# Wider column sums and constant matmuls at the boundaries, and a rearranged start of latent attention, in a fused float32 kernel of six transformer stages and two hybrid layers

## What is computed

```
def modulated_sublayer(x, mod, g_pre, g_post, fn, weight):
    shift, scale, gate = mod[:, 0], mod[:, 1], mod[:, 2]
    h = rmsnorm(x, g_pre) * (1.0 + scale) + shift
    y = rmsnorm(fn(h), g_post)
    return x + weight * (1.0 + gate) * y

def mla_mixer(h, w_in, q_norm, kv_norm, w_uq, w_uk, w_uv, w_o, cos, sin):
    lat = h @ w_in
    c_q, c_kv, k_r = jnp.split(lat, [Q_LORA, Q_LORA + KV_LORA], axis=-1)   # 256, 128, 32 wide
    c_q = rmsnorm(c_q, q_norm)
    c_kv = rmsnorm(c_kv, kv_norm)
    q = jnp.einsum('bsc,chd->bshd', c_q, w_uq)                             # 16 heads
    q_nope, q_rope = q[..., :QK_NOPE], q[..., QK_NOPE:]
    q_rope = apply_rope(q_rope, cos, sin) * ATTN_SCALE
    k_rope = apply_rope(k_r, cos, sin)
    ... scores of q_nope and q_rope against c_kv and k_rope, softmax, values, w_o
```

## Time and profile before

| | |
|---|---|
| runs | 3359.22, 3360.02, 3370.72 us |
| the profiled execution | 3363.93 us; its span 3362.2 us, mean granted clock of TensorE 0.942 |
| TensorE | busy 3128.6 us (93%), 14272 matmul records |
| weight loads of TensorE | 2536.9 us (75%) |
| VectorE | 1700.1 us (51%), 2715 instructions |
| ScalarE | 1158.8 us (34%), 2027 |
| GpSimd | 614.7 us (18%), 359 |
| DMA | 314.07 MB, mean 93 GB/s |
| chain that ended last | TensorE 43%, issue 42%, GpSimd 10%, VectorE 3%, DMA 1% |

### The profile page before, as it was taken

One profiled execution on the slowest core, in us unless ns is written; L12 is line 12 of the kernel. 1 busy time (PEld: TensorE's weight loads), 2 busy tenths in 40 slices (PEclk: granted clock), 3 DMA queues, 4 the chain that ended last, 5 costly groups with the idle time before them and its releaser, 6 DMA issues.

```text
span 3362.2 us, 40116 instructions
## 1 busy us (share of the span) xinstructions
PE 3128.6 (93%) x14272; PEld 2536.9 (75%) x14272; DVE 1700.1 (51%) x2715; ACT 1158.8 (34%) x2027; POOL 614.7 (18%) x359
## 2 busy tenths in 40 slices
PE   6999989999999998688999999996999989879999
PEld 5888878888878887466788877875777878667777
DVE  4554565555564345786511123573666324745653
ACT  2222233222232222465322322534434335344442
POOL 0100000000000000101344443114111331132113
PEclk9999978999999999699899999797999998989999
DMA  5555512555443332101233332013111221121112
GB/s 191 199 174 170 169 61 84 189 179 174 150 146 117 100 107 64 41 13 30 80 94 100 94 107 82 26 44 93 45 38 45 75 82 32 44 81 52 45 38 82
DMA packets 88024, 314.07 MB, mean 93 GB/s; under 512 B 10192, under 2 KB 10960, under 8 KB 87760
## 3 DMA queue, kind: packets, MB, share of 16 engines
q1 hardware_dynamic: 64992, 233.65, 21.9%
q0 software_dynamic: 19488, 71.31, 6.3%
q10 hardware_dynamic: 3408, 7.25, 0.7%
HBM read 307.98 MB, written 2.10 MB: 92 GB/s over the span
## 4 chain that ended last, share of the span: by engine, by line
PE 43%; issue 42%; POOL 10%; DVE 3%; DMA 1%; ACT 0%; POOLq 0%; SPq 0%; ACTq 0%; DVEq 0%
PE psum L377 34%; POOL w_lo L362 10%; PE psum L2044 4%; PE psum L463 1%; PE psum L1055 1%; PE psum L706 1%; DMA ada_first<-ada_in 1%; PE psum L1025 1%; DVE ada_acc L692 1%; PE psum L1988 1%; DMA raw<-stream_in 0%; DVE ta L655 0%; DVE tb L514 0%; DVE h_lo L523 0%; PE psum L938 0%
## 5 line engine op out<-in xcount | busy, mean ns | idle before, releaser
L362 POOL TENSOR_TENSOR w_lo<-raw,w_hi 128x1024 fp32r<-128x1024 f32 x225 | 545.2, 2428 | 1771.1 <-ACT w_hi L333 1589.4
L377 PE MATMUL psum<-h_hi,w_hi 128*128 128x512 f32 x1824 | 506.5, 404 | 36.2 <-DVE h_lo L523 22.9
L377 PE MATMUL psum<-h_hi,w_lo 128*128 128x512 f32 x1824 | 490.2, 395 | 0.0
L377 PE MATMUL psum<-h_lo,w_hi 128*128 128x512 f32 x1824 | 488.7, 394 | 0.0
L377 PEld LDWEIGHTS psum<-h_hi,w_hi 128*128 128x128 f32 x1824 | 349.6, 192 | 126.1 <-DVE h_lo L523 27.9
L377 PEld LDWEIGHTS psum<-h_hi,w_lo 128*128 128x128 f32 x1824 | 347.1, 190 | 75.4
L377 PEld LDWEIGHTS psum<-h_lo,w_hi 128*128 128x128 f32 x1824 | 345.6, 189 | 76.2
L347 ACT ACTIVATE w_hi<-raw 128x1024 fp32r<-128x1024 f32 x256 | 257.9, 1048 | 156.7 <-DMA raw<-stream_in 156.6
L353 DVE TENSOR_TENSOR w_lo<-raw,w_hi 128x1024 fp32r<-128x1024 f32 x192 | 227.8, 1222 | 107.5 <-ACT w_hi L347 101.2
L333 ACT ACTIVATE w_hi<-raw 128x1024 fp32r<-128x1024 f32 x177 | 184.6, 1051 | 219.2 <-PE psum L377 114.9
L832 ACT ACTIVATE a_hi<-tb 128x512 f32 (+1 forms) x88 | 55.6, 632 | 545.3 <-DVE tb L877 545.3
(11 more groups left out here) (404 smaller groups left out, 4874.8 us busy)
## 6 DMA issues: line engine op xcount, KB each, us to landing
raw<-stream_in SPq DMA_DIRECT2D x433, 512.0 KB, 3.6
ada_raw<-ada_in POOLq DMA_DIRECT2D x128, 512.0 KB, 4.7
ada_first<-ada_in POOLq DMA_DIRECT2D x2, 2048.0 KB, 20.5
ada_first<-ada_in SPq DMA_DIRECT2D x2, 2048.0 KB, 25.7
X<-xT_in ACTq DMA_DIRECT2D x1, 2048.0 KB, 9.5
out_x<-X SPq DMA_DIRECT2D x8, 256.0 KB, 2.2
qt_hi<-qr_hi ACTq DMA_DIRECT2D x16, 64.0 KB, 2.1
qt_lo<-qr_lo ACTq DMA_DIRECT2D x16, 64.0 KB, 2.1
```

Of the source, the lines that this page charges most:

```text
L362: pool.tensor_tensor(w_lo[:, u % RING], raw[:, u % RAW], w_hi[:, u % RING].bitcast(F32), ALU.subtract).then_inc(lo_ready, 1)
L377: mm = pe.matmul(dst, w[wi], m[mi], start=(first and n == 0), stop=(last and n == total - 1), skip_group_check=skip)
```

## The change

Three groups of edits.

*Boundaries.* `column_sums` has 64 columns of ones and writes 64 equal columns for each 128 tokens; `sum_columns` reads one of each. VectorE adds the last chunk's product to the others, so that the products need one group of sums, now the last. `keep_busy` issues matmuls of the identity by ones into a bank that nothing reads: 8 between the two spreads and 20 behind the second, after waits for the banks of the next stage. All six boundaries have them.

*Low halves.* GpSimd starts two units later, and at the boundaries into mla, ffn3 and hy0 VectorE makes the two low halves (`early=True`), GpSimd leaves them out.

*Latent attention.* ScalarE writes the zeros, as copies with factor 0, one behind each of the eight h_hi and two after them. The norms are made as at the boundaries: column sums, roots and reciprocals of 128x4, spreads to banks 6 and 5; the fourth latent is copied after the reciprocals. Rotations use banks 7 and 4 in turn, in two rounds of two, and the first q, k and v products are issued after the second rotation matmul.

```
-        def split_lo(dve, u):
-            if u >= own["by_gpsimd"]:
+        def split_lo(dve, u, early=False):
+            if u >= own["by_gpsimd"] and not early:
                 return
...
+        WIDE = 64
+        def column_sums(pe, squares, b, place, first=False):
             for t in range(4):
-                mm = pe.matmul(psum[:, b, column + t:column + t + 1], squares[:, t * P:(t + 1) * P], ones[:, 0:1],
+                at_ = (4 * place + t) * WIDE
+                mm = pe.matmul(psum[:, b, at_:at_ + WIDE], squares[:, t * P:(t + 1) * P], ones[:, 0:WIDE],
                                start=(first and t == 0), stop=True, skip_group_check=True)
+        def keep_busy(pe, b, count):
+            for _ in range(count):
+                pe.matmul(psum[:, b, 0:P], ident[:], ones[:], start=True, stop=True, skip_group_check=True)
...
         def post_pe(pe, L):
+            if L != "pool":
                 pe.wait_ge(gathered.sem, chunks + NC - 1)
                 column_sums(pe, std[:], 4, 0, first=True)
-                column_sums(pe, rstd[:], 7, 4, first=True)
-                column_sums(pe, tb[:, 0], 7, 8)
+                column_sums(pe, tb[:, 0], 7, 1, first=True)
             pe.wait_ge(sq_ready.sem, squares + 2 * NC - 1)
             sums.give(column_sums(pe, last_y, 4, 0), (F, "y"))
+            pe.wait_ge(sq_ready.sem, squares + 2 * NC)
+            column_sums(pe, last_z, 7, 1)
             pe.wait_ge(gathered.sem, chunks + NC)
-            column_sums(pe, tb[:, 1], 7, 4)
-            pe.wait_ge(sq_ready.sem, squares + 2 * NC)
-            sums.give(column_sums(pe, last_z, 7, 8), (F, "z"))
+            sums.give(column_sums(pe, rstd[:], 7, 0), (F, "z"))
             spread_pe(pe, (F, "r"), 2, 6)
+            keep_busy(pe, 5, 8)
             spread_pe(pe, (F, "s"), 5, 5)
+            after = POST[L][3]
+            first = own[after, "ga"] if after in FULL or after == ("hy", 0) else own[after, "g"]
+            for g in range(first, first + 4):
+                pe.wait_ge(sq_ready.sem, squares + 2 * NC)
+                free_bank(pe, g)
+            keep_busy(pe, first % 4, 20)
...
                 if ahead is not None and c in (1, 3):
-                    split_lo(dve, ahead + c // 2)
+                    split_lo(dve, ahead + c // 2, early=True)
...
         def mla_pe(pe, L):
-            norm_pe(pe, (L, "nq"), 2, ones[:])
-            norm_pe(pe, (L, "nkv"), 1, ones[:])
+            for c in range(3):
+                pe.wait_ge(sq_ready.sem, sq_ready.at((L, "n", c)))
+                mm = column_sums(pe, (sq[:, 0], sq[:, 1], ta[:, 0])[c], (4, 4, 7)[c], 0, first=(c != 1))
+                if c:
+                    sums.give(mm, (L, ("nq", "nkv")[c - 1]))
+            spread_pe(pe, (L, "nq"), 2, 6)
+            spread_pe(pe, (L, "nkv"), 5, 5)
...
             for r in range(4):
                 pe.wait_ge(evac.sem, evac.at(("g", g + r)))
-                pe.wait_ge(scaled.sem, scaled.at((L, "rot", r - 1 if r else "k")))
-                sums.give(pe.matmul(psum[:, 5], mconst[:], rotary(r), start=True, stop=True),
+                if r:
+                    pe.wait_ge(scaled.sem, scaled.at((L, "rot", r - 2 if r >= 2 else "k")))
+                sums.give(pe.matmul(psum[:, ROTARY_BANKS[r % 2]], mconst[:], rotary(r), start=True, stop=True),
                           (L, "rot", r))
+                if r == 1:
+                    first_products(pe, "pe", -1)
...
         def mla_act(act, order, L):
+            def zeros(c):
+                tile = (qt_hi, qt_lo, kt_hi, kt_lo)[c // 2]
+                rows, first = ((slice(96, 128), 0), (slice(0, 32), 1))[c % 2]
+                act.activation(tile[rows, first:4:2], ones[rows, 0:1].unsqueeze(2).broadcast_to((32, 2, S)), ACT.Copy, scale=0.0)
+            pre_act(act, L, 12, between=zeros)
...
             split_hi(act, u + 4)
+            for n, b, row in (("nq", 4, 1), ("nkv", 7, 3)):
+                act.wait_ge(sums.sem, sums.at((L, n)))
+                roots.give(act.activation(stat[:, row], sum_columns(b, 0), ACT.Sqrt, bias=eps[:, 0:1]), (L, n))
...
         def mla_dve(dve, order, L):
-            for tile in (qt_hi, qt_lo, kt_hi, kt_lo):
-                order.link(dve.memset(tile[96:128, 0:4:2].bitcast(F32), 0.0))
-                order.link(dve.memset(tile[0:32, 1:4:2].bitcast(F32), 0.0))
-            norm_dve(dve, (L, "nq"))
+            for n, row in (("nq", 1), ("nkv", 3)):
+                dve.wait_ge(roots.sem, roots.at((L, n)))
+                inverses.give(dve.reciprocal(stat[:, row + 1 if row == 1 else 5], stat[:, row]), (L, n))
...
+            for first in (0, 2):
+                by_cosine(first)
+                by_cosine(first + 1)
+                by_sine(first)
+                by_sine(first + 1)
+                for r in (first, first + 1):
+                    split_value_dve(dve, (L, "rot", r), tb[:, r % 2], qr_hi[:, r], qr_lo[:, r])
...
-        own["by_gpsimd"] = own["mla", "u"] + LEAD
+        own["by_gpsimd"] = own["mla", "u"] + 2 * LEAD
...
-            split_lo_gpsimd(pool)
+            lows_gpsimd(pool, own["by_gpsimd"], ahead("mla"))
+            lows_gpsimd(pool, ahead("mla") + 2, ahead("ffn3"))
+            lows_gpsimd(pool, ahead("ffn3") + 2, NU)
```

More of the change, by code:

```diff
@@ L354, in split_lo_loop, with low_gpsimd, lows_gpsimd @@
                               ALU.subtract).then_inc(lo_ready, 1)
-        def split_lo_gpsimd(pool):
-            first = own["by_gpsimd"]
-            def one(i, u):
-                pool.wait_ge(hi_ready, u + 1 if i is None else i * RING + (u + 1))
-                pool.tensor_tensor(w_lo[:, u % RING], raw[:, u % RAW], w_hi[:, u % RING].bitcast(F32),
-                                   ALU.subtract).then_inc(lo_ready, 1)
-            pool.wait_ge(lo_ready, first)
-            rounds = (NU - first) // RING
-            with pool.Fori(0, rounds) as i:
-                for k in range(RING):
-                    one(i, first + k)
-            for u in range(first + rounds * RING, NU):
-                one(None, u)
+        def low_gpsimd(pool, u, i=None):
+            pool.wait_ge(hi_ready, u + 1 if i is None else i * RING + (u + 1))
+            pool.tensor_tensor(w_lo[:, u % RING], raw[:, u % RAW], w_hi[:, u % RING].bitcast(F32),
+                               ALU.subtract).then_inc(lo_ready, 1)
+        def lows_gpsimd(pool, first, end):
+            pool.wait_ge(lo_ready, first)
+            rounds = (end - first) // RING
+            if rounds:
+                with pool.Fori(0, rounds) as i:
+                    for k in range(RING):
+                        low_gpsimd(pool, first + k, i)
+            for u in range(first + rounds * RING, end):
+                low_gpsimd(pool, u)
         def three_passes(pe, dst, weights, moving, first=True, last=True, skip=False):
@@ L508, in pre_act @@
                 part_hi.give(op, (L, c))
+                if between is not None:
+                    between(c)
         def scale_dve(dve, L, c, columns):
@@ L583, in post_chunk_dve @@
                 added = dve.tensor_tensor(rstd[:], rstd[:], tb[:, 1], ALU.add)
-                if L != "pool":
+                if L != "pool" and n < NC - 1:
                     own_order.link(added)
@@ L1192, in plan_mla @@
                 cur.g += 1
-            plan_norm((L, "nq"), 2)
-            plan_norm((L, "nkv"), 1)
+            for c in range(3):
+                sq_ready.plan((L, "n", c))
+            for n in ("nq", "nkv"):
+                for signal in (sums, roots, inverses, spread):
+                    signal.plan((L, n))
+            part_hi.plan((L, "zeros"))
             for c in range(2):
@@ L1388, in mla_extra @@
             return run
+        ROTARY_BANKS = (7, 4)
         def rotary(r):
@@ L1396, in mla_pe @@
             dense_first(pe, L, u, g, 4)
-            norm_pe(pe, (L, "nq"), 2, ones[:])
-            norm_pe(pe, (L, "nkv"), 1, ones[:])
+            for c in range(3):
+                pe.wait_ge(sq_ready.sem, sq_ready.at((L, "n", c)))
[4 more added lines that the diff above has]
+            spread_pe(pe, (L, "nkv"), 5, 5)
             pe.wait_ge(stage_loaded, own[L, "loaded"])
             pe.wait_ge(evac.sem, evac.at(("g", g + 3)))
-            sums.give(pe.matmul(psum[:, 5], mconst[:], lat[:, 3], start=True, stop=True), (L, "rot", "k"))
+            sums.give(pe.matmul(psum[:, 4], mconst[:], lat[:, 3], start=True, stop=True), (L, "rot", "k"))
             u, g = u + 4, g + 4
```

77 lines of the change are left out of this document (42 added, 35 removed).

## The result

The changed kernel takes 3320.57 us (median of 4 runs, 3314.66 to 3328.2) against 3359.62 us of the kernel before (4 runs): a ratio of 0.9885, 95% interval 0.9863 to 0.9907. The forecast was 3323. The profiled execution took 3322.28 us, its span 3320.6.

A forecast was written before the change was run, and what follows sets the result against it. TensorE is busy nearly throughout; time is to be had where it waits or runs at 1.2 GHz. Boundaries 13.3, second hybrid layer 3.0, pool stage 0 and latent attention 21.5 sum to 37.8 us: forecast 3323 us, range 3300 to 3344.

The forecast's parts named there:

- Sums: Five boundaries: five groups of 64-column sums hold the clock and take 4.4 us each; 12.2 us gained.
- Filler and spreads: Boundaries: 8 and 20 constant matmuls cost nothing; first spread no longer runs behind, 0.3 us each, 1.5 us in five.
- Low halves: Boundaries into latent attention, ffn3, first hybrid layer: 7.2 us saved without GpSimd, 7.3 given back by VectorE; zero.
- Boundaries in sum: Boundaries: 12.2 + 1.5 + 0, less 0.4 for TensorE's cold start at ffn3's boundary, 13.3 us gained.
- Pool stage: Pool stage: the clock still falls in the wait before its first sums and stays at 1.2 GHz; zero gained.
- Rival 2: Pool stage keeps its clock: 19 us more there and 4 at its boundary, 3299 us; chance 0.08.
- Second hybrid layer: Second hybrid layer: its 64 records of sums take 7.1 us instead of 10.18 at held clock; 3.0 us gained.
- Latent attention: Start of latent attention: zeros, small norms and two-bank rotations bring scores at d + 40.8 instead of d + 62.5; 21.5 us.
- 1: Boundaries and second hybrid layer: 64-column sums lose the clock as single columns do, gaining 0; 3341 us; chance 0.15.
- the slower rival: Six boundaries: filler at 1.2 GHz stands ahead of real work, first product 9 us late; 3381 us; chance 0.03.
- 3: Same as the slower rival: half-clock boundary filler delays real work, 48 us at six boundaries; 3381 us; chance 0.03.
- 4: Latent attention's gain is overtaken by loads or GpSimd, 10 us less; 3333 us; chance 0.06.

The follow-up runs named there:

- run 1: The changed kernel without the 8 and 20 constant filler matmuls at all six boundaries: 3314.11 us.
- run 2: The changed kernel with column sums one column wide instead of 64, filler kept: 3337.64 us.
- run 3: The changed kernel with column sums 16 columns wide instead of 64: 3336.66 us.
- run 7: The changed kernel with the low halves at the boundaries into latent attention, ffn3 and the first hybrid layer made by GpSimd again: 3323.01 us.
- run 8: The changed kernel with 9 more constant matmuls (18 records) ahead of the pool stage's first column sums: 3302.97 us, median of three; a fourth run took 5084.96 us.
- run 4: The changed kernel with the start of latent attention put back as before the change, boundaries as changed: 3344.96 us.
- run 5: The changed kernel with latent attention's zeros written by VectorE memsets again: 3324.82 us.
- run 6: The changed kernel with latent attention's rotations one at a time in one bank, first q, k and v products behind the last: 3322.29 us.
- run 10: The changed kernel with filler at pool, latent attention and hybrid waits, including 8 and 37 in the pool's first products, and four transfers behind the second rotation: 3290.33 us.
- run 12: The changed kernel with filler at pool, latent attention (38 matmuls ahead of scores) and hybrid waits, four transfers moved, no boundary filler: 3285.09 us.

## Why the prediction was right

- **Sums: right.** Forecast 4.4 us each and 12.2 us in five boundaries; measured 4.57 and 34.16 - 22.86 = 11.3. The choice that carried it, that 64 columns hold the clock, is shown by runs 1 to 3.
- **Filler and spreads: right, "costs nothing".** The first product does come 1.4 us later than without filler, and TensorE has caught up as forecast. It gains nothing either. The 0.3 us per boundary that I drew from the first spread moving up came: behind ffn0 and ffn1 the first h_lo is done 6.6 us after the end of the sums before and 6.3 us after the change.
- **Low halves: right against the kernel before, and 2.4 us in the changed one.** The forecast was zero, 7.2 us saved and 7.3 given back. First and last h_lo of each boundary, in us after its first sum (read from VectorE's timelines):

```
behind   sums end         first h_lo               last h_lo
         before  after    before  after  run 7     before  after  run 7
ffn0      8.25    4.57    14.82   10.85  10.85     31.82   27.85  27.85
ffn1      7.19    4.57    13.75   10.84  10.84     33.04   30.12  30.12
ffn2      5.84    4.57    14.69   10.85  13.86     31.69   30.12  30.86
mla       7.35    4.57    15.38   10.85  13.86     32.38   30.13  30.86
ffn3      5.55    4.57    14.61   10.79  13.80     31.01   29.46  30.21
```

  Before, GpSimd's low halves made the first h_lo late by 2.3, 1.5 and 2.5 us behind ffn2, mla and ffn3 (its distance to the end of the sums is 8.9, 8.0 and 9.1 us against 6.6 elsewhere): 6.2 us together, where I had 7.2. VectorE's own halves give back 2.3 us per boundary, from the first h_lo to the last: 6.8. Net, 0.6 us lost. Run 7 shows 2.4 us gained because it stands against the changed kernel: there the sums are shorter, VectorE's chain falls fully beside GpSimd's operations in all three places, and the first h_lo is 3.0 us late in each. Had GpSimd kept the low halves, part of what the shorter sums gain would have gone that way.
- **Boundaries in sum:** forecast 13.3. Read by the 192nd record or the next sums, the five gained 3.4 (behind ffn0), 2.9, 1.6, 2.6 and 1.8 us, 12.3 in all. The parts make the same: 11.3 in the sums, 1.5 in the first spread, 0.6 lost in the low halves. The sums, mis-sized by 0.9, are most of what is missing. The 0.4 us that I took off for a cold start of TensorE were not lost: behind mla and ffn3 the 192nd record gained 0.3 to 0.4 us more than the last h_lo did.
- **Pool stage: right as forecast (0), with the rival's price confirmed.** The clock fell before its first sums as before. Rival 2's mechanism, put in by hand in run 8, gave 20.7 us, boundary included, where I had worked out 19 and 4 for the boundary.
- **Second hybrid layer: direction right, size not.** Forecast 3.0; by its 192nd record 5.3 us were gained (62.6 to 57.3 us after the first sum): 2.6 in the sums, 0.9 in the spread, 1.4 in the wait for the first h_lo, and the rest in first products of which fewer run at half clock. That third part is the step I had wrong: I had the first h_lo bound by GpSimd's low halves and moving with them, without a gain, but it took 1.03 us instead of 2.40. VectorE, before and after:

```profile
2693.79 2.40 DVE L521 TENSOR_TENSOR h_lo<-tb,h_hi 128x512 fp32r<-128x512 f32 x1
```

```profile
2647.26 1.03 DVE L536 TENSOR_TENSOR h_lo<-tb,h_hi 128x512 fp32r<-128x512 f32 x1
```

  By the end of the layer the 5.3 us had all gone. Across seven traces with identical code in it (the changed kernel and runs 1 and 4 to 8) this layer took 672.9 us (82 cold) to 684.9 us (103 cold), the first hybrid layer 669.2 to 678.9: the fall of the clock in them differs from run to run, and this trace had a long one. So a gain of 5 us inside them can't be read from one trace.
- **Latent attention: right to 3 us.** Products on cq 13.0 us earlier relative to d (forecast 12.5), kt_hi 17.9 (17.2), cosine 17.9 (17.2), rotations 14.1 us long (15.5), scores 24.0 us earlier (21.5). The whole was confirmed by run 4. One step was not in the sum: between the rotations and the scores I had only the splits of q and k, 5.5 us; the 5.4 us measured hold ScalarE's four issues of transfers, 2.5 us, as well.
- **Rivals.** 1 was priced at 3341; one column measures 3337.6, with the filler late as the slower rival had it, by 1.6 us behind latent attention instead of the 9 us it priced. 3 didn't happen in the changed kernel, but its mechanism is real on a smaller scale (runs 2 and 10). 4 did not appear: scores moved with the chain.
- **The skill's rule on transposes.** The filler's 18 records in run 8 held the clock, and in run 12 the clock stayed at 1.00 through 76 of them, 8.65 us: ordinary matmuls with the identity as an operand keep it up. The trace that I had set against the rule was weak evidence: in those 20 us of attention 31 of 97 records are transposes (L1025), and the products beside them can have held the clock. The Trainium skill, page "TensorE: Matmul & The Clock Gate", Part 4, excludes transpose-mode only; no run here used that as filler.

The sum, 37.8 us, stands against 39.05 by medians and 41.6 by the two spans. That it came so close is partly luck: the scores of latent attention moved 2.5 us more than forecast, the boundaries gained 1.0 us less, and of the second hybrid layer's 3.0 us none is left at its end in this trace. The choices that carried the forecast (64 columns hold the clock, the pool stage stays at half clock, the parts of latent attention chain as worked out) were not luck: runs 1 to 4 and 8 and the rows of latent attention bear them out.

## What to carry to other kernels

A short wait of TensorE can cost far more than itself, if the work behind it does not bring the clock back, as the pool stage's did not for 44.4 us: look for stages that stay at 0.50 with TensorE busy, and bridge the wait in front of them (18 records bought 20.7 us), not the waits in front of wide products (the boundaries' filler bought nothing). Give tiny matmuls more columns when they cost the same: forty records took 4.52 us with one column and 4.57 us with 64, both at full clock. Filler stands in an in-order queue: cut it to the wait, and cut it again whenever something upstream moves.

## What was not expected

- A wait of 1.39 us decided 44 us of clock: the pool stage stayed at 0.50 for 44.4 us after it, with TensorE busy all the time, and at 1.00 throughout once it was bridged.
- Sixteen columns lose the clock as one does (3336.7 and 3337.6 us), though all three widths take 4.5 to 4.6 us for the five groups at full clock.
- A higher granted clock (0.82 to 0.93 over 120 us of a hybrid layer) was worth only a few us, and a quarter of TensorE's busy time in that stretch was the filler that bought it.
